# Five edits of order in a two-block kernel: the recurrence's convolution, the first output products, the modulation bias, the rotary work, and the odd layer's value accumulators

## The reference, cut to what matters

```python
# first block: recurrence branch
xr = causal_depthwise_conv(xr, conv_w, conv_b)            # 4 taps
gate_r = einsum(xr, wa) + ba; gate_i = einsum(xr, wx) + bx
log_a = 8 * sigmoid(gate_r) * log_sigmoid(lam)
# first block: output
y = concatenate([rms_norm(y_a), rms_norm(y_b), rms_norm(y_c)])
x = x + y @ w_out
h2 = rms_norm(x); x = x + hierarchical_moe(h2, ...)
# second block, every layer: modulation
shift, scale, gate = split(silu(cond) @ ada_w + ada_b, 3)
# even layer: latent attention
q_nope, q_rope = split(rms_norm(cq) @ w_uq); q_rope = apply_rope(q_rope)
k_nope, v = split(rms_norm(ckv) @ w_ukv)
s = (q_nope @ k_nope + q_rope @ k_rope) * scale; o = softmax(s) @ v
y_mla = o * silu(mg)
# odd layer
f, f_gate, u, v, s_gate = split(modulate(x) @ w_in)
vg = layer_norm(gelu(v))                                  # per 128 channels
y_s = gelu(u) * (sgu_w @ vg + sgu_b) * silu(s_gate)
y_f = real(fft2(f)) * silu(f_gate)
```

## Time and profile before

| | |
|---|---|
| median of 3 runs | 2398.38 us (2397.45 to 2401.68) |
| the profiled execution's own time | 2392.42 us |
| its span in the trace | 2390.6 us |
| mean granted clock of TensorE | 0.976 |
| TensorE, VectorE, ScalarE, GpSimd busy | 94%, 64%, 49%, 16% |

### The profile page before, as it was taken

The page is one execution under the profiler, slowest core; times in us unless marked ns, Lnnn a source line. Parts: engine busy times, 40 slices in busy tenths (PEclk is TensorE's granted clock), DMA queues, the critical chain, the costliest instruction groups (busy, mean ns, idle before and its releaser), DMA issues. The chain is left out here.

```text
span 2390.6 us, 27110 instructions
## 1 busy us (share of the span) xinstructions
PE 2245.7 (94%) x10870; PEld 1688.7 (71%) x10870; DVE 1527.5 (64%) x1882; ACT 1179.1 (49%) x1670; POOL 379.1 (16%) x272
## 2 busy tenths in 40 slices
PE   7999998997899999999979999988999998899998
PEld 6867755673688888888768777744555486788876
DVE  5777387436799999999872265566555457423475
ACT  3256367501688888887753244354444513302321
POOL 2000022000211111111100000013555532000014
PEclk9999999998899999999989999999999999999999
DMA  3201010219999999999752101130000112111231
GB/s 125 67 22 53 1 71 1 84 66 404 341 373 383 382 383 404 389 395 382 296 207 77 47 14 37 36 108 0 1 36 18 72 78 81 54 53 36 93 127 53
DMA packets 107419, 349.85 MB, mean 146 GB/s; under 512 B 23644, under 2 KB 55205, under 8 KB 79256
## 3 DMA queue, kind: packets, MB, share of 16 engines
q1 hardware_dynamic: 94856, 322.72, 36.2%
q0 software_dynamic: 11232, 21.09, 2.4%
q10 hardware_dynamic: 1200, 4.24, 0.4%
HBM read 327.38 MB, written 37.40 MB: 153 GB/s over the span
## 5 line engine op out<-in xcount | busy, mean ns | idle before, releaser
L230 PE MATMUL psm<-r,r 128*128 128x512 f32 (+3 forms) x7294 | 1748.3, 397 | 62.2 <-DVE r L343 13.8
L230 PEld LDWEIGHTS psm<-r,r 128*128 128x128 f32 (+2 forms) x7294 | 1357.5, 190 | 419.2 <-issue 66.4
L343 DVE TENSOR_TENSOR r<-mem,r 128x1024 fp32r<-128x1024 f32 (+1 forms) x456 | 526.9, 1203 | 143.0 <-ACT r L334 137.5
L334 ACT ACTIVATE r<-mem 128x1024 fp32r<-128x1024 f32 (+1 forms) x456 | 442.7, 1037 | 53.1 <-DMA mem<-in_w_in_dram 22.3
L230 PE MATMUL psm<-mem 128*64 128x128 f32 (+12 forms) x2230 | 340.8, 424 | 19.9 <-DVE mem L870 5.5
L230 PEld LDWEIGHTS psm<-mem 128*64 128x64 f32 (+6 forms) x2230 | 171.5, 161 | 145.4 <-issue 107.5
L3427 POOL TENSOR_TENSOR mem<-mem 128x1024 f32<-128x1024 f32 x63 | 152.5, 2421 | 163.9 <-ACT mem L3379 106.6
L3379 ACT ACTIVATE mem<-psm 128x512 f32<-128x512 f32 x160 | 94.4, 596 | 141.5 <-PE psm L230 134.8
L3213 DVE TENSOR_REDUCE small<-psm 128x1 f32<-128x1280 f32 x64 | 95.3, 1489 | 89.0 <-PE psm L230 89.0
L265 ACT ACTIVATE small<-small 128x1 f32<-128x1 f32 (+3 forms) x26 | 7.7, 295 | 225.6 <-DVE small L380 151.4
L3551 POOL TENSOR_TENSOR mem<-mem 128x1024 f32<-128x1024 f32 x14 | 33.6, 2400 | 405.4 <-ACT mem L3518 405.4
(11 more groups left out here) (342 smaller groups left out, 1743.3 us busy)
## 6 DMA issues: line engine op xcount, KB each, us to landing
mem<-in_exp_w_gate_dram SPq DMA_DIRECT2D x64, 1024.0 KB, 7.4
mem<-in_exp_w_up_dram SPq DMA_DIRECT2D x64, 1024.0 KB, 7.6
mem<-in_exp_w_down_dram SPq DMA_DIRECT2D x64, 1024.0 KB, 7.3
mem<-in_ada_w_dram SPq DMA_DIRECT2D x16, 1024.0 KB, 14.3
mem<-in_odd_w_in_dram SPq DMA_DIRECT2D x10, 1024.0 KB, 5.4
mem<-in_x_dram SPq DMA_DIRECT2D x16, 512.0 KB, 7.1
mem<-in_w_in_dram SPq DMA_DIRECT2D x8, 1024.0 KB, 5.4
mem<-in_ada_w_dram SPq DMA_DIRECT2D x16, 512.0 KB, 14.5
```

The costliest lines, as they stand in the source:

```text
L230: return p.e.matmul(o, l, r, start=start, stop=stop, skip_group_check=True)
L334: p.e.activation(h, mem(self.raw(i), [R * n])[:, w * q:w * q + w], ACT.Copy).then_inc(*self.hi_done.up(i, q))
L343: p.e.tensor_tensor(l, mem(self.raw(i), [R * n])[:, w * q:w * q + w], h.bitcast(F32), SUB).then_inc(*self.lo_done.up(i, q))
```

## The change

It moves work between places in the streams and changes two bank orders; what is computed stays the same.

- Recurrence: ScalarE takes its two steps at (j 1, half 1) and (j 2, half 1), VectorE at j == 2; TensorE keeps j == 3.
- First output products: TensorE waits for the low part of each row in turn, and VectorE makes the low parts of rows 4 and 5 before it scales rows 6 and 7.
- Bias: it gets memory of its own, and its load goes ahead of the second norm's weights.
- Rotary work: the two entries of the first rotary group go ahead of the first keys and queries; Silu goes behind the entry of the third pair's keys.
- Odd layer: two banks for transpositions, six for value tiles; the third weight piece is split on ScalarE behind the fourth Gelu, on VectorE ahead of the statistics.

```diff
@@ project_scalar
-                    run(lru, j == 3)
+                    run(lru, (j, half) in ((1, 1), (2, 1)))
@@ project_vector
-                    run(lru, j == 3)
+                    run(lru, j == 2)
@@ w_out_tensor
-            p.wait_ge(*on_dve.at("lo", 0, 7))
             for i in range(3):
                 for q in range(2):
-                    w_out_part(p, i, q, own, take(p, "wo", i, q), True, False)
+                    ps = take(p, "wo", i, q)
+                    for j in own:
+                        p.wait_ge(*on_dve.at("lo", 0, j))
+                        w_out_part(p, i, q, (j,), ps, j == own[0], False)
@@ w_out_vector
+            out_lo_vector(p, 0, 0)
             out_rows_vector(p, 0, 1)
-            for t in range(2):
-                out_lo_vector(p, 0, t)
+            out_lo_vector(p, 0, 1)
@@ modulation
-        BIA = mem(62, [512], p=12)
+        BIA = mem(193.5, [512], p=12)
@@ ada_sync, behind ada_fetch(p, 1)
+            p.e.dma_start(BIA, A["ada_b_2"].rearrange("l (h n) -> (l h) n", n=512)).then_inc(*bias_in.up())
@@ norm2_sync, at its end
-            p.e.dma_start(BIA, A["ada_b_2"].rearrange("l (h n) -> (l h) n", n=512)).then_inc(*bias_in.up())
@@ latent attention
-        UP = [("qr", 0, 0), ("qr", 0, 1), ("kn", 0, 0), ("qn", 0, 0), ("rope", 0, 0), ("rope", 0, 1), ("kn", 1, 0), ("qn", 1, 0),
+        UP = [("qr", 0, 0), ("qr", 0, 1), ("rope", 0, 0), ("rope", 0, 1), ("kn", 0, 0), ("qn", 0, 0), ("kn", 1, 0), ("qn", 1, 0),
@@ up_scalar, behind the first query copies
-                    if a == 0:
-                        p.wait_ge(*mg_back.at())
-                        for j in range(4):
-                            p.e.activation(MG[:, j, :], MG[:, j, :], ACT.Silu).then_inc(*up_act.up("mg", j))
-                        p.e.preload_act_table_set(LN_EXP)
@@ up_scalar, at the end of an entry
                 first_scalar(p, UP.index((name, a, b)) - 6)
+                if UP.index((name, a, b)) == 8:
+                    gates_silu_scalar(p)
+        def gates_silu_scalar(p):
+            p.wait_ge(*mg_back.at())
+            for j in range(4):
+                p.e.activation(MG[:, j, :], MG[:, j, :], ACT.Silu).then_inc(*up_act.up("mg", j))
+            p.e.preload_act_table_set(LN_EXP)
@@ odd layer
-        TURN, VALUE = (0, 1, 2, 3), (4, 5, 6, 7)
+        TURN, VALUE = (0, 1), (4, 5, 6, 7, 2, 3)
@@ odd_scalar
-                if i == 5:
+                if i == 3:
                     WD.split_scalar(p, 2)
@@ odd_vector
             p.then(p.e.memset(FO[:, :, 0:1], 0.0), od_dve, "fo0")
+            WD.split_vector(p, 2)
             for i in range(8):
...
-                if i == 5:
-                    WD.split_vector(p, 2)
```

## The result

The changed kernel takes 2379.95 us (median of 4 runs, 2379.38 to 2380.51) against 2397.91 (4 runs, 2397.33 to 2401.68): a ratio of 0.9924 [0.9910, 0.9939], 18.0 us less. The forecast was 2385.2 (2376 to 2392), 13.2 us less. The direction and the range held, and 2379.95 lies at the fast edge of the 2380 to 2390 that I thought likeliest; two terms of the sum did not hold. One execution of before took 7600.8 us at a mean granted clock of 0.351; it is left out of every ratio and range.

What follows compares the result with a forecast made beforehand. TensorE, busy 94% of the span, was taken as the bound, with gains only from its 145 us of standing still and the slow clock after stops. Terms 7.9 + 2.6 + 0.7 + 0 + 2 = 13.2 us gave 2385.2, range 2376 to 2392.

Steps and rivals of the forecast that it cites:

- A: Recurrence's convolution made sooner: 5.25 us of TensorE's stop plus 2.6 of slow products behind it, 7.9 us (5.2 to 8.3).
- B: First output products taken row by row as low parts finish: computed 3.3 to 3.8 us sooner, taken as 2.6 (1.4 to 4.2).
- C: Modulation bias loaded earlier: its 3.99 us wait goes, but the saturated transfer stream leaves only 0.7 us (0 to 4.0).
- D: Latent attention, rotary work first: the first score product stays where it was, bound by VectorE; 0 us (-2 to 4.7).
- E: Odd layer, six value accumulators and two transposition banks: 5.3 + 2.0 - 4.7 = 2.6 us, taken as 2 (-1 to 7).
- the Gelu wait: Odd layer, TensorE's 3.60 us wait on the first Gelu: shrinks by about 1.5, its slow clock by 0.5.
- TensorE's warm arrival: Latent attention, first score product: TensorE would get there warmer, worth 1 to 2 us; query banks up to 0.7 late.
- The banks: Odd layer, transpositions in two banks instead of four: the seventh waits, costing 3.7 us and about 1 of slow clock.
- the last stop: Odd layer, before the first channel product: the earlier weight split removes 3.77 us and about 1.5 of slow clock, 5.3.
- the return in full: Rival, chance 0.15: C and D return their whole waits (3.3 and 4.7 more), two banks cost nothing; any two give about 2377.
- No other stop took A's place: Rival at the convolution, chance 0.14: late fifth weight piece's low parts or key norms; A returns about 4, total 2389.
- the slower rival: Odd layer, chance 0.03: two banks make twelve transpositions wait 1.5 us each, 18 us, ending at 2403.

## Why the prediction was right, and where it was not

Undone one by one, the parts are worth 7.6 (A), 2.9 (B), -0.5 (C), 4.4 (D) and 3.5 us (E), 17.9 together, beside the 18.0 measured. The forecast had 7.9, 2.6, 0.7, 0 and 2. That the five meet the 18.0 so closely is luck: each is uncertain by about 2 us, and if each is instead the 18.0 less what the run still gains over before on its own chip, they make 9.5, 4.7, -0.2, 4.7 and 5.3, 24 together. By the traces the runs without A, B, C and D each carry the 1.5 us of slow products behind the Gelu wait, which is no part's own. The range was wide enough to hold a term of the sum that had failed.

- **A** was right in both steps: the stop, and the slow products behind it. (Its upper bound does not follow: without overlap the 28 products take 7.9 us instead of 7.3, and A would be 7.2, not 8.3.)
- **B**: computed at 3.3 to 3.8, and the stage shows 3.7. I reduced it for the slow clock; that reduction failed in the trace, though the medians leave 2.9. The window over the stage reads 1.00 for the granted clock, with both waits in it:

```profile
427.00:437.00 10.00, 8.18 (x28) 5.07 (x28) 6.25 (x9) 7.12 (x12) 0.00 (x0) 1.00 0.73 273
```

  Waits of 1.45 and 1.00 us cost no clock here, and the one wait of 4.25 did (12 products in 5.22 us with B undone). The Trainium skill ("TensorE: Matmul & The Clock Gate", section "HAM oscillation — how this bites in real kernels") tells of a kernel whose bursts of products are each followed by a wait of about 3 to 5 us on a transfer and start slow every time. This stage agrees: only its long wait did that. (At the Gelu, a wait of 2.11 us was followed by slow products in eight profiles of eleven.)
- **C** was right as far as these runs can tell: the saturated stream takes back what the bias gave.
- **D** is the step that failed: "D: 0". Its pieces were right (the first score product where it was, the rotary blocks stretched, the copies at 10.65 where I had 10.8). What I priced at 1 to 2 us and then cancelled against a late Silu was TensorE's warm arrival. It measures 2.8 us against the run without D (1592.94 against 1590.13) and 1.5 against before, so the price was fair and the cancelling was wrong. The late Silu cost 0.3: a few products later, six take 2.6 us in nearly all kernels with the late Silu and 2.31 in those without. The medians' 4.4 is more than the traces give to D; 1.5 of it lies behind the Gelu wait.
- **E** had the right three terms, and the second was too small: the Gelu wait returned 2.9 us for my 2.0, because in this profile it had no slow products behind it. That was luck: the wait shrank by 1.5, as computed, and eight of eleven profiles do have them. The banks cost 3.6 where I had 4.7, and the last stop gave 4.0 and the slow products behind it 1.6, near my 5.3. I took 2 where the terms made 2.6; the medians say 3.5, the traces 4.9, or 3.4 with slow products behind the Gelu wait.

Of the rivals, the return in full did not come about: C's wait went to the transfers and D's to the rotary work, and the two banks cost nearly what I said. No other stop took A's place, and of the twelve transpositions that the slower rival has waiting, one cost time, by 7.68 us.

The base was mis-set as well. I took 13.2 off a median that lay 6.0 us above the profile, as if that distance were fixed. It is no property of the program: in the changed kernel the profile and the median differ by 0.5. That it goes with the clock is shown by the correlation; which stretches cost it in the runs without a profile, and why the clock falls there, stays open.

That VectorE and GpSimd stretch each other is a rule of the Trainium skill too ("SBUF — State Buffer", section "Who interferes with whom"): a VectorE instruction with two inputs in SBUF reads the second through ports that it shares with GpSimd, and so contends with a GpSimd instruction that reads SBUF. The run with the copies moved agrees: 0.69 against 1.62 us, 8.42 against 10.65.

## What to carry to other kernels

A stop costs its length and what the slow clock takes behind it, so a stop moved to an earlier place, where other work sets the pace, can pay although the next milestone starts no sooner: that was 1.5 to 2.8 us of D. Look at what runs beside a short chain on another engine: holding back GpSimd's copies, and placing the wait for them where it is needed, was worth 5.6 us by the medians, more than any edit but A. A profile is one draw of a time that scatters, so take a small term from runs with and without it; and where two profiles differ, see at which instruction they part, because the difference need not lie at the edit.

## What was not expected of the hardware

The same wait of 2.11 us on the Gelu was followed by six products in 1.7 us in three profiles and in 2.8 to 2.9 in eight, among them kernels whose odd layer is the same. The granted clock also fell in stretches with no idle time above 0.20 us near, as at 1400 us above (0.79 over 8 us; twelve products took 4.61 us that took 3.04 in before). Such a stretch costs 1.6 us. That one and its like near 1447 us stand behind four products of 16 rows each and came together, in six of the fourteen profiles: both of the changed kernel, those without C, D and E, and that with the Silu alone moved; neither of before has them. What sets them off is open. Beside one another on one chip, before scattered over 8 us (9 runs) and the changed kernel over 4 (5 runs), but the kernel with the later copies over 6.6 (5 runs).
